# Rows spread over the partitions by a selector matmul and a VectorE copy instead of a DRAM round trip, in the mLSTM phase of a two-layer mixer

## The chip, the core and the metric

The program runs on one core of one Trainium2 chip. The metric is the device time of one execution, in microseconds. TensorE is the matmul engine (PE in the rows, its weight loads PEld), VectorE is DVE, ScalarE is ACT, GpSimd is POOL, and SyncE (SP) issues the DMAs.

## The reference, cut to what matters

The model has 512 tokens and 1024 channels. Its first mixer holds an mLSTM with 4 heads and a gated delta rule with 4 heads, both chunked; the input projections of both come from one normalised input. What the change touches are rows with one number for each head and token (4 x 512), which every partition needs:

```
b = jnp.cumsum(lf_, -1)                                     # mLSTM, log forget gates
log_d = where(causal, b[..., :, None] - b[..., None, :] + ig_[..., None, :], -inf)
m_t = jnp.maximum(jnp.max(log_d, -1), b + m[..., None])      # running maximum
d = jnp.exp(log_d - m_t[..., None])
...
G = jnp.cumsum(to_chunks(g, L), -1)                          # delta rule, log decays
decay = where(incl, exp(G[..., :, None] - G[..., None, :]), 0.0)
a_mat = where(strict, bc[..., :, None] * kk * decay, 0.0) + eye(L)   # bc = beta
```

The kernel computes with the token index on the free axis, so `d` and `decay` need a row of M (the running maximum), G and beta on all 128 partitions.

## The kernel before, in words

The program is a sequence of phases, each a block of five instruction streams that ends in a barrier: input loads and norm, `mlstm`, `delta`, the output projection, a feed-forward phase, a second mixer and its feed-forward phase, and a third layer. Nothing of a phase starts before every engine has left the one before. The order on each engine is the order in which the code is written; engines wait for each other by semaphores.

A projection of 128 output channels is 8 units of three matmuls each (`product`, L187 to L189: the fp32 weight and input are split into a high and a low part), 128x512 each. The split of the weight is a ScalarE copy (L151) and a subtraction on GpSimd or VectorE (L160); the 512 KB weight tile comes by SP's queue into a ring of four.

`mlstm` works head by head. In `body(h)` TensorE makes the attention scores of head h (`score`, L1619, banks b4 and b5), multiplies them with the values (`numerator`, L1626), turns tiles with 128x128 transposes (L204), and between these works through 24 units (16 from head 2 on) of the projections of later heads; `fill(n)` takes the next n units. VectorE takes the projections out of PSUM, weighs the scores (L1872), makes the arguments of the decays from the row M (`arguments`, L1864), and after a head takes its output (`out`, L1896). ScalarE exponentiates the arguments (L1719), GpSimd masks them (L1802).

The gate rows are made at the start of the phase as tiles of 4 partitions (`gate_rows`: M, G, beta). Head 0's row of M is spread to 128 partitions by TensorE: `spread_row` (L1604) multiplies a selector of ones with the four rows into a bank, and `take_m` (L1857) copies the bank to `m_M`. The rows of M for heads 1 to 3 and all rows of G and beta go through DRAM: SP's queue stores them to `row_scratch` (L1562, L1566, L1568) and loads them back with the partition axis broadcast (L1554), M into `m_M_next`, G and beta into `delta_bc`, which the `delta` phase reads. `turn_rows` (L1600) also turns G and beta into columns (`gate_cols`), from which L1926 to L1928 and L1931 make decay columns, with two ScalarE exponentials (L1765, L1766).

Of the kernel before, what the change touches and what calls it, by code (L numbers as in the profile page):

```python
# [86 lines left out]
class Core:  # L87
# [33 lines left out]
    def sem(self, name):  # L121
        self.sems.append(self.nc.alloc_semaphore(name))
        return self.sems[-1]
# [1371 lines left out]
def mlstm(k, weights, ahead):  # L1495
# [14 lines left out]
    acc, vraw, on, bcm = (sb(f"m_{s}", [P, T], F32) for s in "acc v_raw on M".split())  # L1510
    bcms = sb("m_M_next", [P, H - 1, T], F32)
    rows = nc.dram_tensor("row_scratch", (3 * HA, T), F32).ap()
    (rows_out, m_in, gb_in) = (sem("row_" + s) for s in ("out", "m_in", "gb_in"))
    q, kk = (sb(f"m_{s}", [DK, T], F32) for s in "q k".split())
# [10 lines left out]
    gb = lambda i: k.p("gbias", i)[0:HA]  # L1525
    (raw_taken, if_ready, tanh_done, f_soft, ab_taken, a_soft, b_ready, m_rows, g_rows, m_turned, m_cols, e_ready, g_turned,
     cols_ready, cols_exp, cols_done) = (sem("ab_" + s) for s in (
         "raw_taken if_ready tanh_done f_soft ab_taken a_soft b_ready m_rows g_rows m_turned m_cols e_ready g_turned "
         "cols_ready cols_exp cols_done").split())
    (qk_taken, og_taken, v_taken, v_turned, v_ready, v_ones, tapped, convolved, qk_ready, og_clamped, og_ready, m_spread, bcm_ready, arg_ready, d_ready,  # L1530
     d_masked, st_done, wt_ready, num_done, den_taken, squared, tot_ready, on_scaled, o_turned, y_ready, ch_act, ch_dve, ch_pool) = (sem("m_" + s) for s in (
         "qk_taken og_taken v_taken v_turned v_ready v_ones tapped convolved qk_ready og_clamped og_ready m_spread bcm_ready arg_ready d_ready "
         "d_masked st_done wt_ready num_done den_taken squared tot_ready on_scaled o_turned y_ready ch_act ch_dve ch_pool").split())

    def cs(c):
# [12 lines left out]
    with nc.Block() as block:  # L1548
        @block.sync
        def _(sp):  # L1550
            def spread_rows(out, kind, first, done):
                n = HA - first
                src = rows[kind * HA + first:(kind + 1) * HA, :].rearrange("(a h) t -> a h t", a=1).to_broadcast([P, n, T])
                sp.dma_start(out, src).then_inc(done, 16)  # L1554

            for h in range(2, H):
                for s in range(3):
                    k.wait_split(sp, 3 * h - 3 + s)
                    k.load(sp, s, weights[3 * h + s, :, :])
                if h == 2:  # L1560
                    sp.wait_ge(m_rows, 1)
                    sp.dma_start(rows[0:HA, :], r_M).then_inc(rows_out, 16)  # L1562
                    sp.wait_ge(rows_out, 16)
                    spread_rows(bcms[:, :, :], 0, 1, m_in)
                    sp.wait_ge(g_rows, 1)
                    sp.dma_start(rows[HA:2 * HA, :], r_G).then_inc(rows_out, 16)  # L1566
                    sp.wait_ge(b_ready, 1)
                    sp.dma_start(rows[2 * HA:3 * HA, :], r_b).then_inc(rows_out, 16)  # L1568
                    sp.wait_ge(rows_out, 48)
                    spread_rows(k.bcg[:, 0, :, :], 1, 0, gb_in)  # L1570
                    spread_rows(k.bcg[:, 1, :, :], 2, 0, gb_in)
            k.wait_split(sp, 3 * H - 1)
            k.load_ahead(sp, ahead, upto=3 * H)

        @block.tensor
        def _(pe):
# [52 lines left out]
            def body(h):  # L1629
                n, f = h + 1, h + 2  # L1630
                slots = {H: (0, 1), H + 1: (2, 3)}.get(f, (0, 1, 2))
                units = [(min(f, H), s, m) for s in slots for m in range(KD)]

                def fill(count):
                    for _ in range(min(count, len(units))):
                        g, s, m = units.pop(0)
                        project(g, s, m, m + 1)

                pe.wait_ge(qk_ready, h + 1)
                if h == 0:  # L1640
                    pe.wait_ge(bcm_ready, 1)
                if h == 1:
                    pe.wait_ge(cols_ready, 1)
                if h:
                    pe.wait_ge(y_ready, h - 1)
                score(h, 0)
                score(h, 1)
                fill(3)
                score(h, 2)
                score(h, 3)  # L1650
                fill(3)
                pe.wait_ge(v_ready, h + 1)
                if h:
                    pe.wait_ge(on_scaled, h)
                if h == 0:
                    pe.wait_ge(m_cols, 1)
                    pe.wait_ge(v_ones, 1)
                numerator(h, 0)
                numerator(h, 1)
                fill(2)  # L1660
                numerator(h, 2)
                numerator(h, 3).then_inc(num_done, 1)
                if n < H:
                    turn_v(n)
                if h:
                    turn_o(h - 1)
                fill(4)
                if h == 0:
                    pe.wait_ge(g_rows, 1)
                    pe.wait_ge(b_ready, 1)  # L1670
                    turn_rows(b4, (r_G, r_b)).then_inc(g_turned, 1)
                fill(len(units))

# [13 lines left out]
        def _(act):  # L1687
# [50 lines left out]
            def body(h):  # L1738
# [22 lines left out]
                if f < H:  # L1761
                    high(f + 1, 0)
                if h == 2:
                    act.wait_ge(cols_done, 1)
                    nc.scalar.activation(k.cols[:, 3, :, :], k.cols[:, 3, :, :], ACT.Exp)  # L1765
                    nc.scalar.activation(k.cols[:, 4:6, :, :], k.cols[:, 4:6, :, :], ACT.Exp, scale=-1.0).then_inc(cols_exp, 1)  # L1766
# [56 lines left out]
        def _(dve):  # L1823
# [30 lines left out]

            def take_m():
                dve.wait_ge(m_spread, 1)
                nc.vector.tensor_copy(bcm[:, :], b4[:, :]).then_inc(bcm_ready, 1)  # L1857

            def arguments(h):

                dve.wait_ge(*((m_in, 16) if h else (bcm_ready, 1)))
                m = bcms[:, h - 1, :] if h else bcm
                for j in range(NT):
                    ins = nc.vector.tensor_scalar(Ws[h % 2][:, off[j]:off[j + 1]], m[:, j * P:T], mcols[:, 0, h, j:j + 1], 0.0, ALU.subtract, ALU.max)  # L1864
                ins.then_inc(arg_ready, 1)
# [32 lines left out]
            def body(h):  # L1898
# [13 lines left out]
                take_den(h)  # L1912
                if n < H:
                    arguments(n)
                totals(h)
                if h:
                    out(h - 1)
                if h == 0:
                    dve.wait_ge(g_turned, 1)
                    t = b4[:, 0:2 * NT * HA].rearrange("p (k c h) -> p k h c", k=2, c=NT)  # L1920
                    nc.vector.tensor_copy(k.cols[:, 1:3, :, :], t).then_inc(cols_ready, 1)
                if h == 1:
                    dve.wait_ge(gb_in, 32)
                    dve.wait_ge(cols_ready, 1)
                    last = k.bcg[:, 0, :, :].rearrange("p h (c l) -> p h c l", l=P)[:, :, :, P - 1]
                    nc.vector.tensor_copy(k.cols[:, 5, :, :], last)  # L1926
                    ch.link(nc.vector.tensor_tensor(k.cols[:, 3, :, :], k.cols[:, 1, :, :], last, ALU.subtract))
                    nc.vector.tensor_copy(k.cols[:, 4, :, :], k.cols[:, 1, :, :]).then_inc(cols_done, 1)  # L1928
                if h == 3:
                    dve.wait_ge(cols_exp, 1)  # L1930
# [25 lines left out]
            dve.wait_ge(m_cols, 1)  # L1956
            take_m()
            arguments(0)
# [1324 lines left out]
```

## Time and profile before

| what | value |
|---|---|
| time, median of 3 runs | 1823.6 us (1821.07 to 1826.46) |
| time of the profiled execution | 1823.6 us |
| span of the profiled execution (first to last instruction) | 1821.8 us |
| TensorE busy | 1727.1 us, 95% |
| VectorE, ScalarE, GpSimd busy | 1080.8, 853.9, 428.9 us |
| TensorE clock granted, mean | 0.984 of full |
| the `mlstm` phase in the span | about 36 to 139 us |

A busy share is an average over all phases; what counts for the change is which engine sets the pace between 36 and 139 us. Matmuls are pipelined: their rows overlap, and the distance between two starts is what a matmul costs, not the duration in its row. A row's duration includes the time until the result has landed.

### The profile page before, as it was taken

The numbers are of one execution on the slowest core, as the hardware profiler recorded it, in microseconds if no ns is written. First come the engines' busy times: TensorE is split into PE (matmuls) and PEld (weight loads), VectorE is DVE, ScalarE is ACT, GpSimd is POOL, SyncE is SP. The second block draws the span as 40 slices with busy tenths as digits, with TensorE's granted clock in tenths as the row PEclk, the third lists the DMA queues.
The fourth block names the chain that finished last, engine by engine and source line by source line (L and its number), as shares of the span: only waits on it lengthen the run. The fifth ranks groups of instructions, "written<-read, shape, count | busy, mean of one in ns | idle before, by whom it ended". The sixth has DMA issues, their size and how long they took to land. (4 is left out here: it accounts for less than half of the span.)

```text
span 1821.8 us, 23819 instructions
## 1 busy us (share of the span) xinstructions
PE 1727.1 (95%) x8324; PEld 1394.1 (77%) x8324; DVE 1080.8 (59%) x1694; ACT 853.9 (47%) x1452; POOL 428.9 (24%) x332
## 2 busy tenths in 40 slices
PE   7998998989999999889999999999999989898997
PEld 5776887878888888768888877888888766666665
DVE  5536454377656633777887858566643475776243
ACT  5656445354333323565565645333332452445653
POOL 0434444101111100145555500111100111222222
PEclk9999999999999999999999999999999999999999
DMA  5311102223222222212212121323232320211111
GB/s 204 118 58 70 35 36 64 70 75 105 94 102 92 94 100 94 81 58 70 70 47 70 59 92 58 104 92 99 73 115 94 112 74 12 81 47 47 59 69 46
DMA packets 40360, 143.19 MB, mean 79 GB/s; under 512 B 4556, under 2 KB 4812, under 8 KB 39896
## 3 DMA queue, kind: packets, MB, share of 16 engines
q1 hardware_dynamic: 40280, 142.14, 23.0%
q8 instruction: 49, 0.80, 0.2%
q14 instruction: 31, 0.25, 0.0%
HBM read 140.00 MB, written 2.12 MB: 78 GB/s over the span
## 5 line engine op out<-in xcount | busy, mean ns | idle before, releaser
L187 PE MATMUL bank<-u_high,w_high 128*128 128x512 f32 x1580 | 650.6, 412 | 24.3 <-POOL w_low L160 10.0
L189 PE MATMUL bank<-u_high,w_low 128*128 128x512 f32 x1580 | 622.3, 394 | 0.0
L188 PE MATMUL bank<-u_low,w_high 128*128 128x512 f32 x1580 | 621.7, 393 | 0.0
L187 PEld LDWEIGHTS bank<-u_high,w_high 128*128 128x128 f32 x1580 | 300.6, 190 | 107.4 <-issue 31.7
L189 PEld LDWEIGHTS bank<-u_high,w_low 128*128 128x128 f32 x1580 | 299.7, 190 | 65.7
L151 ACT ACTIVATE w_high<-w_ring 128x1024 fp32r<-128x1024 f32 x233 | 244.0, 1052 | 221.4 <-PE bank L189 167.6
L188 PEld LDWEIGHTS bank<-u_low,w_high 128*128 128x128 f32 x1580 | 301.0, 191 | 58.4 <-issue 3.8
L160 DVE TENSOR_TENSOR w_low<-w_ring,w_high 128x1024 fp32r<-128x1024 f32 x176 | 220.9, 1258 | 178.3 <-ACT w_high L151 178.0
L160 POOL TENSOR_TENSOR w_low<-w_ring,w_high 128x1024 fp32r<-128x1024 f32 x57 | 135.7, 2391 | 532.7 <-ACT w_high L151 532.7
L881 ACT ACTIVATE conv_up<-bank,col_sb 128x512 f32<-128x512 f32 x88 | 68.6, 779 | 270.6 <-DVE bank L936 270.6
L996 POOL TENSOR_TENSOR hidden<-conv_up 128x512 f32 x44 | 58.2, 1323 | 494.0 <-DVE conv_up L947 373.8
L936 DVE TENSOR_TENSOR bank<-bank,root_in 128x512 f32<-128x512 f32 x88 | 61.4, 698 | 134.2 <-PE bank L189 133.5
L187 PE MATMUL bank<-src_high_down,w_high 128*128 128x512 f32 x352 | 137.5, 391 | 2.3 <-DVE src_low_down L479 2.3
L188 PE MATMUL bank<-src_low_down,w_high 128*128 128x512 f32 x352 | 137.2, 390 | 0.0
L189 PE MATMUL bank<-src_high_down,w_low 128*128 128x512 f32 x352 | 137.1, 390 | 0.0
L1319 POOL TENSOR_TENSOR c_X<-c_k,c_dif 128x256 f32<-128x256 f32 x56 | 60.0, 1071 | 150.9 <-ACT c_dif L1210 150.9
L187 PEld LDWEIGHTS bank<-src_high_down,w_high 128*128 128x128 f32 x352 | 66.1, 188 | 17.5 <-issue 2.2
L189 PEld LDWEIGHTS bank<-src_high_down,w_low 128*128 128x128 f32 x352 | 66.1, 188 | 13.7
L188 PEld LDWEIGHTS bank<-src_low_down,w_high 128*128 128x128 f32 x352 | 66.1, 188 | 13.5
L946 DVE SCALAR_TENSOR_TENSOR conv_up<-bank,col_sb,conv_up 128x511 f32<-128x511 f32 x88 | 65.9, 749 | 15.5 <-ACT conv_up L881 11.9
L947 DVE SCALAR_TENSOR_TENSOR conv_up<-bank,col_sb,conv_up 128x510 f32<-128x510 f32 x88 | 65.9, 749 | 10.1 <-DVE conv_up L946 0.3
L1354 DVE TENSOR_TENSOR c_dif<-c_G 128x512 f32<-128x512 f32 x56 | 54.5, 997 | 24.9 <-PE bank L1116 24.4
(414 smaller groups left out, 2294.8 us busy)
## 6 DMA issues: line engine op xcount, KB each, us to landing
w_ring<-ffn_up SPq DMA_DIRECT2D x88, 512.0 KB, 3.4
w_ring<-ffn_down SPq DMA_DIRECT2D x44, 512.0 KB, 3.4
w_ring<-c_in SPq DMA_DIRECT2D x32, 512.0 KB, 3.5
w_ring<-g_in SPq DMA_DIRECT2D x16, 512.0 KB, 3.6
w_ring<-m_in SPq DMA_DIRECT2D x12, 512.0 KB, 6.3
w_ring<-fox_in SPq DMA_DIRECT2D x12, 512.0 KB, 3.5
w_ring<-dsa_in SPq DMA_DIRECT2D x12, 512.0 KB, 3.4
w_ring<-ab_out SPq DMA_DIRECT2D x8, 512.0 KB, 4.1
```

The lines of the kernel that those rows point to most:

```text
L151: self.nc.scalar.activation(self.ws[s][0][:, :], self.w[:, s, :], ACT.Copy).then_inc(self.w_high, 1)
L160: eng.tensor_tensor(low[:, :], self.w[:, s, :], high[:, :].bitcast(F32), ALU.subtract).then_inc(self.w_split, 1)
L187: nc.tensor.matmul(out, a[0], b[0], start=start, stop=False)
L188: nc.tensor.matmul(out, a[0], b[1], start=False, stop=False)
L189: return nc.tensor.matmul(out, a[1], b[0], start=False, stop=stop)
L881: nc.scalar.activation(cg[:, s, :], bank(i, s)[:, :], ACT.Identity, bias=coef(4 * i + s, 3), scale=coef(4 * i + s, 2)).then_inc(tap_done, 1)
L936: nc.vector.tensor_tensor(bank(i, s)[:, :], bank(i, s)[:, :], k.rn[:, :], ALU.mult).then_inc(taken, 1)
L946: ch.link(nc.vector.scalar_tensor_tensor(cg[:, s, 1:T], bank(i, s)[:, 0:T - 1], coef(4 * i + s, 1), cg[:, s, 1:T], ALU.mult, ALU.add))
L947: nc.vector.scalar_tensor_tensor(cg[:, s, 2:T], bank(i, s)[:, 0:T - 2], coef(4 * i + s, 0), cg[:, s, 2:T], ALU.mult, ALU.add).then_inc(con ...
L996: nc.gpsimd.tensor_tensor(h[:, bass.ds(2 * i + s // 2, 1), :], cg[:, s - 1:s, :], cg[:, s:s + 1, :], ALU.mult).then_inc(mul_done, 1)
L1319: nc.gpsimd.tensor_tensor(x[:, :, 0, :], blocks(kk[:, :], b)[:, :, 0, :], d[:, :, 0, :], ALU.mult)
L1354: nc.vector.tensor_tensor(dif[:, l % R, :].rearrange("p (n b) -> p n b", b=2 * b), g, ref, ALU.subtract).then_inc(diff_ready, 1)
```

## The change

The DRAM scratch, SP's six DMAs on it with their three semaphores, and the tile `m_M_next` are gone. In their place:

- rows of M: after the last numerator of head h TensorE spreads the row of head h+1 into bank b5, and VectorE copies it to `m_M` before it makes the arguments;
- rows of G and beta: each of the 8 is spread into b4 or b5 by TensorE near the end of a body, behind two units of `fill`, and copied to `delta_bc` by VectorE: four rows in head 0 (all of G), two in head 1 and two in head 2;
- the next head's first scores wait until the last copy has left the bank (`spread_used`);
- the decay columns are made one head earlier on VectorE and ScalarE.

The core of the diff. In order: SP, the lists, TensorE in `body(h)` (ahead of the scores, behind the last numerator, ahead of the last fill), ScalarE's exponentials of the columns, VectorE:

```diff
-                if h == 2:
-                    sp.wait_ge(m_rows, 1)
-                    sp.dma_start(rows[0:HA, :], r_M).then_inc(rows_out, 16)
-                    sp.wait_ge(rows_out, 16)
-                    spread_rows(bcms[:, :, :], 0, 1, m_in)
...
-                    spread_rows(k.bcg[:, 0, :, :], 1, 0, gb_in)
-                    spread_rows(k.bcg[:, 1, :, :], 2, 0, gb_in)
...
+    spreads = {0: [(0, h) for h in range(H)], 1: [(1, 0), (1, 1)], 2: [(1, 2), (1, 3)], 3: []}
+    used = {h: sum(len(spreads[g]) for g in range(h)) for h in range(H + 1)}
...
-                if h == 0:
-                    pe.wait_ge(bcm_ready, 1)
-                if h == 1:
-                    pe.wait_ge(cols_ready, 1)
+                pe.wait_ge(bcm_ready, h + 1)
+                pe.wait_ge(spread_used, used[h])
...
                 if n < H:
+                    pe.wait_ge(wt_ready, NT * h + NT)
+                    spread_row(b5, r_M, n).then_inc(m_spread, 1)
...
+                for i, (kind, g) in enumerate(spreads[h]):
+                    fill(2)
+                    if i == 0:
+                        pe.wait_ge(*((y_ready, h) if h else (cols_ready, 1)))
+                    elif i == 1:
+                        pe.wait_ge(bcm_ready, n + 1)
+                    else:
+                        pe.wait_ge(spread_used, used[h] + i - 1)
+                    spread_row(b_s[i % 2], (r_G, r_b)[kind], g).then_inc(spread, 1)
                 fill(len(units))
...
-                if h == 2:
+                if h == 1:
...
-            def take_m():
-                dve.wait_ge(m_spread, 1)
-                nc.vector.tensor_copy(bcm[:, :], b4[:, :]).then_inc(bcm_ready, 1)
+            def take_m(h):
+                dve.wait_ge(m_spread, h + 1)
+                nc.vector.tensor_copy(bcm[:, :], (b5 if h else b4)[:, :]).then_inc(bcm_ready, 1)
...
                 if n < H:
+                    take_m(n)
                     arguments(n)
...
-                if h == 1:
-                    dve.wait_ge(gb_in, 32)
-                    dve.wait_ge(cols_ready, 1)
+                for i, (kind, g) in enumerate(spreads[h]):
+                    dve.wait_ge(spread, used[h] + i + 1)
+                    nc.vector.tensor_copy(k.bcg[:, kind, g, :], b_s[i % 2][:, :]).then_inc(spread_used, 1)
+                if h == 0:
+                    dve.wait_ge(spread_used, H)
```

TensorE, the last part of body(2) in the kernel before, from the last numerator of head 2 to the first scores of head 3 (L1626 numerator, L204 transposes, L187 a unit's first matmul, L1619 scores):

```order
L1626 MATMUL bank7<-m_v0,x_res 128x129 x3
L204 MATMUL bank2<-cst_sb,m_v_raw 128x128 [waits m_v_taken]
...
L204 MATMUL bank4<-cst_sb,m_on 128x128 [waits m_y_ready,m_on_scaled]
...
L187 MATMUL bank1<-u_high,w1_high 128x512 [waits m_og_taken,w_split]
...
L1619 MATMUL bank4<-m_q,m_k 128x512 [waits m_y_ready,m_qk_ready]
L1619 MATMUL bank5<-m_q,m_k 128x384
```

The same place in the changed kernel, whose line numbers are others (L1608 numerator, L1586 `spread_row`, L1601 scores):

```order
L1608 MATMUL bank7<-m_v0,x_res 128x129 x3
L1586 MATMUL bank5<-gate_rows,cst_sb 128x512 [waits m_wt_ready]
L204 MATMUL bank2<-cst_sb,m_v_raw 128x128 [waits m_v_taken]
...
L204 MATMUL bank4<-cst_sb,m_on 128x128 [waits m_y_ready,m_on_scaled]
...
L187 MATMUL bank1<-u_high,w1_high 128x512 [waits m_og_taken,w_split]
...
L1586 MATMUL bank4<-gate_rows,cst_sb 128x512 [waits m_y_ready]
...
L1586 MATMUL bank5<-gate_rows,cst_sb 128x512 [waits m_bcm_ready]
L1601 MATMUL bank4<-m_q,m_k 128x512 [waits ab_spread_used,m_y_ready,m_bcm_ready,m_qk_ready]
L1601 MATMUL bank5<-m_q,m_k 128x384
```

Eight units (24 matmuls) stood between the transposes and the scores; now six stand before the first of the two spreads, two between them, and none behind the second, so that the scores' wait for `spread_used` follows it directly. In heads 0 and 1 four and eight units stand behind the last spread.

VectorE behind head 0 in the kernel before (L1877 takes the denominators, L1864 makes the arguments of head 1):

```order
L1877 COPY m_den<-bank7 128x2
L1864 TENSOR_SCALAR x_res<-m_M_next,m_cols 128x512 [waits row_m_in]
L1864 TENSOR_SCALAR x_res<-m_M_next,m_cols 128x384
L1864 TENSOR_SCALAR x_res<-m_M_next,m_cols 128x256
L1864 TENSOR_SCALAR x_res<-m_M_next,m_cols 128x128
```

And in the changed kernel (L1868, L1849 `take_m`, L1855 the arguments, L1916 the copies to `delta_bc`):

```order
L1868 COPY m_den<-bank7 128x2
L1849 COPY m_M<-bank5 128x512 [waits m_m_spread]
L1855 TENSOR_SCALAR x_res<-m_M,m_cols 128x512 [waits m_bcm_ready]
...
L1913 COPY gate_cols<-bank4 128x32 [waits ab_g_turned]
L1916 COPY delta_bc<-bank4 128x512 [waits ab_spread]
L1916 COPY delta_bc<-bank5 128x512 [waits ab_spread]
L1916 COPY delta_bc<-bank4 128x512 [waits ab_spread]
L1916 COPY delta_bc<-bank5 128x512 [waits ab_spread]
L1920 COPY gate_cols<-delta_bc 128x16 [waits ab_spread_used]
```

A copy that waits for the spread now stands ahead of the arguments, and four copies ahead of the column work.

## Rows read from the trace of the kernel before

**Rows 1.** The page: busy time, share, instructions of each engine.
```profile
PE 1727.1 (95%) x8324; PEld 1394.1 (77%) x8324; DVE 1080.8 (59%) x1694; ACT 853.9 (47%) x1452; POOL 428.9 (24%) x332
```
**Rows 2.** Busy time by stretch: us, engines' busy (instructions), TensorE clock, DMA share.
```profile
core 0: us, PE busy (x) PEld busy (x) DVE busy (x) ACT busy (x) POOL busy (x), PEclk, DMA share, GB/s
57.50:81.30 23.80, 22.94 (x113) 17.87 (x112) 9.49 (x22) 14.87 (x29) 13.71 (x9) 1.00 0.41 155
81.30:103.80 22.50, 22.50 (x109) 17.81 (x108) 9.19 (x25) 13.60 (x27) 8.86 (x7) 1.00 0.34 117
103.80:120.80 17.00, 17.00 (x85) 13.31 (x84) 8.82 (x22) 13.28 (x29) 6.47 (x6) 1.00 0.10 32
139.00:300.00 161.00, 146.39 (x907) 125.42 (x908) 82.89 (x140) 87.28 (x197) 75.09 (x69) 0.99 0.13 47
```
**Rows 3.** Timeline of TensorE, end of `mlstm`: start us, us, instruction, idle before.
```profile
137.47 0.60 PE L204 MATMUL bank<-cst_sb,m_on 128*128 128x128 f32 x4
139.25 0.47 PE L187 MATMUL bank<-u_high,w_high 128*128 128x512 f32 x1 [1.18 <-PEq L1548]
```
**Rows 4.** Timeline of SP's queue and of VectorE, the DRAM way and its readers.
```profile
57.01 0.82 SPq L1554 DMA_DIRECT2D delta_bc<-row_scratch  x2
60.17 5.23 SPq L127 DMA_DIRECT2D w_ring<-m_in  x3
...
69.32 0.23 DVE L1877 COPY m_den<-bank 128x2 f32<-128x2 f32 x2 [2.68 <-PE bank L1626]
69.47 1.26 DVE L1864 TENSOR_SCALAR x_res<-m_M_next,m_cols 128x512 f32<-128x512 f32 x4
```
**Rows 5.** Timeline of TensorE, the spread of head 0's row.
```profile
47.68 1.12 PE L1604 MATMUL bank<-gate_rows,cst_sb 4*128 4x512 f32 x2 [0.22 <-DVE gate_rows L1947]
48.64 0.60 PE L1600 MATMUL bank<-cst_sb,gate_rows 4*128 4x4 f32 x8
```
**Rows 6.** Timeline of TensorE, scores of head 1 between two units.
```profile
80.84 0.39 PE L188 MATMUL bank<-u_low,w_high 128*128 128x512 f32 x1
81.07 0.39 PE L189 MATMUL bank<-u_high,w_low 128*128 128x512 f32 x1
81.39 1.77 PE L1619 MATMUL bank<-m_q,m_k 64*128 64x512 f32 x4
83.09 0.50 PE L187 MATMUL bank<-u_high,w_high 128*128 128x512 f32 x1
83.42 0.40 PE L188 MATMUL bank<-u_low,w_high 128*128 128x512 f32 x1
```
**Rows 7.** Timelines of TensorE and VectorE: a result, its reader, a copy from PSUM.
```profile
72.42 0.65 PE L1600 MATMUL bank<-cst_sb,gate_rows 4*128 4x4 f32 x8
...
73.11 0.19 DVE L1921 COPY gate_cols<-bank 128x32 f32<-128x32 f32 x1 [1.72 <-PE bank L1600]
...
46.95 0.68 DVE L1947 TENSOR_TENSOR gate_rows<-gate_rows 4x512 f32<-4x512 f32 x1
...
50.31 0.69 DVE L1857 COPY m_M<-bank 128x512 f32<-128x512 f32 x1
```
**Rows 8.** Timelines of GpSimd and VectorE: slack behind heads 0 and 2.
```profile
72.57 1.70 POOL L1802 TENSOR_TENSOR x_res<-x_res,cst_sb 128x128 f32<-128x128 f32 x4 [7.53 <-ACT x_res L1719]
...
82.62 0.69 DVE L1872 SCALAR_TENSOR_TENSOR x_res<-bank,x_res 128x512 f32<-128x512 f32 x1 [9.31 <-PE bank L1619]
...
122.16 1.16 DVE L1872 SCALAR_TENSOR_TENSOR x_res<-bank,x_res 128x512 f32<-128x512 f32 x2 [4.29 <-PE bank L1619]
```
**Rows 9.** Timelines of TensorE and GpSimd: the one stall inside the heads.
```profile
60.20 0.50 PE L187 MATMUL bank<-u_high,w_high 128*128 128x512 f32 x1 [0.86 <-POOL w_low L160]
...
53.70 2.63 POOL L1802 TENSOR_TENSOR x_res<-x_res,cst_sb 128x128 f32<-128x128 f32 x4 [10.12 <-ACT x_res L1719]
```
**Rows 10.** Timeline of TensorE at the start of `mlstm`: matmuls at the lower clock.
```profile
37.14 0.77 PE L187 MATMUL bank<-u_high,w_high 128*128 128x512 f32 x1 [3.25 <-DVE m_on L1934]
...
40.22 0.40 PE L188 MATMUL bank<-u_low,w_high 128*128 128x512 f32 x1
```

More of the change, by code:

```diff
@@ L1510, in mlstm @@
     acc, vraw, on, bcm = (sb(f"m_{s}", [P, T], F32) for s in "acc v_raw on M".split())
-    bcms = sb("m_M_next", [P, H - 1, T], F32)
-    rows = nc.dram_tensor("row_scratch", (3 * HA, T), F32).ap()
-    (rows_out, m_in, gb_in) = (sem("row_" + s) for s in ("out", "m_in", "gb_in"))
     q, kk = (sb(f"m_{s}", [DK, T], F32) for s in "q k".split())
@@ L1525, in mlstm @@
     gb = lambda i: k.p("gbias", i)[0:HA]
-    (raw_taken, if_ready, tanh_done, f_soft, ab_taken, a_soft, b_ready, m_rows, g_rows, m_turned, m_cols, e_ready, g_turned,
+    (raw_taken, if_ready, tanh_done, f_soft, ab_taken, a_soft, b_ready, m_rows, g_rows, m_turned, m_cols, e_ready, g_turned, spread, spread_used,
      cols_ready, cols_exp, cols_done) = (sem("ab_" + s) for s in (
-         "raw_taken if_ready tanh_done f_soft ab_taken a_soft b_ready m_rows g_rows m_turned m_cols e_ready g_turned "
+         "raw_taken if_ready tanh_done f_soft ab_taken a_soft b_ready m_rows g_rows m_turned m_cols e_ready g_turned spread spread_used "
          "cols_ready cols_exp cols_done").split())
@@ L1550, in _ @@
         def _(sp):
[L1551 to L1554, printed above, removed]
             for h in range(2, H):
@@ L1559, in _ @@
                     k.load(sp, s, weights[3 * h + s, :, :])
-                if h == 2:
-                    sp.wait_ge(m_rows, 1)
-                    sp.dma_start(rows[0:HA, :], r_M).then_inc(rows_out, 16)
-                    sp.wait_ge(rows_out, 16)
-                    spread_rows(bcms[:, :, :], 0, 1, m_in)
[L1565 to L1569, printed above, removed]
-                    spread_rows(k.bcg[:, 0, :, :], 1, 0, gb_in)
-                    spread_rows(k.bcg[:, 1, :, :], 2, 0, gb_in)
             k.wait_split(sp, 3 * H - 1)
@@ L1663, in body @@
                 if n < H:
+                    pe.wait_ge(wt_ready, NT * h + NT)
+                    spread_row(b5, r_M, n).then_inc(m_spread, 1)
+                if n < H:
                     turn_v(n)
@@ L1853, in convolve @@
                 ins.then_inc(convolved, 1)
-            def take_m():
-                dve.wait_ge(m_spread, 1)
-                nc.vector.tensor_copy(bcm[:, :], b4[:, :]).then_inc(bcm_ready, 1)
+            def take_m(h):
+                dve.wait_ge(m_spread, h + 1)
+                nc.vector.tensor_copy(bcm[:, :], (b5 if h else b4)[:, :]).then_inc(bcm_ready, 1)
             def arguments(h):
-                dve.wait_ge(*((m_in, 16) if h else (bcm_ready, 1)))
-                m = bcms[:, h - 1, :] if h else bcm
+                dve.wait_ge(bcm_ready, h + 1)
                 for j in range(NT):
-                    ins = nc.vector.tensor_scalar(Ws[h % 2][:, off[j]:off[j + 1]], m[:, j * P:T], mcols[:, 0, h, j:j + 1], 0.0, ALU.subtract, ALU.max)
+                    ins = nc.vector.tensor_scalar(Ws[h % 2][:, off[j]:off[j + 1]], bcm[:, j * P:T], mcols[:, 0, h, j:j + 1], 0.0, ALU.subtract, ALU.max)
                 ins.then_inc(arg_ready, 1)
@@ L1928, in body @@
                     nc.vector.tensor_copy(k.cols[:, 4, :, :], k.cols[:, 1, :, :]).then_inc(cols_done, 1)
-                if h == 3:
+                if h == 2:
                     dve.wait_ge(cols_exp, 1)
@@ L1956, in _ @@
             dve.wait_ge(m_cols, 1)
-            take_m()
+            take_m(0)
             arguments(0)
```

## The prediction

> **What bounds the kernel now.** I read the page first: TensorE is busy 1727.1 of 1821.8 us, 95%, and no other engine passes 59% [rows 1]. That is an average over eleven phases, so the busy time by stretch comes next, cut at the first scores of each head. In the stretches of heads 0 to 2 TensorE is busy 22.94 of 23.80, 22.50 of 22.50 and 17.00 of 17.00 us, at full clock; VectorE is busy for less than half of the first two and 8.82 of 17.00 in the third [rows 2]. The reader is to see that in the place of the change TensorE has no hole to put work in: two stretches of the three have none, the first has one stall of 0.86 us, ahead of all added work but not made by it [rows 9].
>
> The timeline then says who wants what the DRAM way delivers. The broadcast of G and beta is issued at 57.01 and the M rows are there when VectorE turns to them: it makes the arguments at 69.47, right behind the denominators, with no wait for a DMA [rows 4]. The SP queue, free of these DMAs at 57.83, next issues a weight load at 60.17, and that one waits for a split. It follows GpSimd's low part, not the row DMAs. So what is removed is hidden entirely, and what is added lies mainly on the engine that sets the pace.
>
> **What is removed.** Six DMAs on SP's queue, worth nothing: nobody is seen waiting for them, and SP is held by the weight splits anyway [rows 4]. One possible gain is left: their traffic may slow other engines. GpSimd's first mask took 2.63 us against 1.70 us in the next head [rows 8, 9], and the stall of 0.86 us waits for GpSimd's work behind it. VectorE was busy with the gate rows at that moment too, so I take 0 and keep -0.86 us as the end of the range.
>
> **One spread on TensorE.** Two matmuls of 512 columns, 4 partitions deep. Head 0's spread stands in the trace: it starts at 47.68 and the next instruction at 48.64, so it costs 0.96 us inside a run of plain fp32 matmuls [rows 5]. Between units of projections the change of kind costs too. The scores of head 1 start 0.32 us after the unit matmul before them, where units follow each other at 0.23 us: 0.09 us. The second matmul behind the scores comes at 0.33 us: 0.10 us [rows 6]. An isolated spread is 0.96 + 0.19 = 1.15 us. Below, it can't be less than the 0.96 us of the row, as long as it runs; above, I use its 1.12 us from start to the landed result, if nothing of it overlapped, plus 0.19, so 1.31 us.
>
> - The three M spreads (heads 1 to 3) stand between the numerator and the transposes, fp32 on both sides: 3 x 0.96 = 2.88 us.
> - Of the eight spreads of G and beta, seven stand alone between units (four in head 0, two in head 1, the first in head 2): 7 x 1.15 = 8.05 us.
> - The eighth stands directly ahead of the scores of head 3 and shares their entry: 0.96 us.
>
> **The waits added.** Behind the eighth spread no unit is left. The scores wait for `spread_used`, so: the result lands 1.12 us after the spread's start, VectorE sees it 0.04 us later (73.07 to 73.11), the copy takes 0.69 us, and TensorE starts 0.05 us after VectorE ends (47.63 to 47.68) [rows 5, 7]. That makes 1.90 us after the spread's start, where the scores could have started at 0.96: a new stall of 0.94 us. Below it is 0; above 1.90 us. Queued behind this wait are the scores of head 3 and all units after them, so nothing covers it.
>
> The other waits I cost at nothing. Two units, six matmuls at 0.23 us, are 1.4 us between spreads, more than the 0.94 us that the copy lags, and a bank is used again only at the second next spread. Behind the last spread of heads 0 and 1 stand four and eight units. The wait for `y_ready` has six units ahead of it. If one of these covers were gone, it would cost up to 0.94 us each.
>
> **VectorE, ScalarE, GpSimd.** VectorE gets 11 copies of 0.69 us, 7.6 us in all, into stretches where it waits 9.31 us ahead of the first weighing of head 1 and 4.29 us ahead of that of head 3 [rows 7, 8]. The M copy stands ahead of the arguments: at latest it ends at 69.32 + 1.12 + 0.04 + 0.69 = 71.17, so the arguments come 1.7 us later, and the exponentials and the mask with them. The mask of head 1 ended at 74.27 and is wanted at 82.62, which itself moves out by more than 5 us [rows 4, 8]. Nothing is late there: 0.
>
> **The sum.** 2.88 + 8.05 + 0.96 + 0.94 = 12.8 us, against the profiled execution's own 1823.6 us (span 1821.8 and 1.8 around it), which is also the median of the three runs. `mlstm` ends with TensorE's last transposes at 137.47, VectorE's output behind them, and a barrier; TensorE starts again at 139.25 [rows 3]. All phases behind it move out by the same amount: 1836.4 us.
>
> **The rivals.**
>
> *The clock falls.* Eleven more changes of kind, one new stall, and spreads that use four partitions of 128. For it: before `mlstm` TensorE stood still for 3.25 us, and its next eight starts, 37.14 to 40.22, took 3.08 us for seven distances that are 1.6 us at 0.23: the lower level, 1.2 GHz, for 1.5 us of loss [rows 10]. Against it: after the idle stretches of 0.86 and 1.18 us the next unit matmuls come at full clock, and heads 0 to 2 show 1.00 throughout, with four or more such groups in each [rows 2, 3, 9]. One spell in each of three heads: 12.8 + 4.5 = 17.3, 1840.9 us. The Trainium skill (TensorE: Matmul & The Clock Gate, "A second HAM failure mode: psum-queue depth-cycling") warns that short idle moments between groups of matmuls that cycle through PSUM banks can make the clock swing between its levels; that speaks against this change, and the granted clock of 1.00 in heads that already cycle through eight banks does not bear it out.
>
> *The copies are always late.* If VectorE reaches each spread late, or a wait costs TensorE its run-ahead, each of the seven other spreads exposes 0.94 us: 12.8 + 6.6 = 19.4, 1843.0 us. For it: VectorE runs in order and the copies stand behind totals and output. Against it: the 9.31 us of slack, and 1.4 us between two spreads.
>
> *Not slower: the end of `mlstm` isn't TensorE's.* If another engine comes last to the barrier by 12.8 us or more, the added work vanishes under it, and the stall of 0.86 us may go with the DMAs: 1823.6 - 0.9 = 1822.7 us. It decides at the barrier, at the point where that engine's lateness equals the sum. For it: 14.6 us of the 161 us behind are idle on TensorE, so something else is waited for in `delta` [rows 2]. Against it: the only work between 137.47 and 139.25 hangs on TensorE's own transposes, and units of the next projection follow at once [rows 3]. Idle time behind a barrier covers nothing ahead of it.
>
> **How the numbers follow.** The forecast has 80%, the clock 8%, the late copies 6%, the covered end 6%. For the range: the low end has eleven spreads at 0.96, no new stall and the old one gone, 10.56 - 0.86 = 9.7 us; the high end eleven at 1.31 and 1.90 of stall, 16.3 us. With the 2.9 us by which runs of the kernel before lie around their median, that is 1830.4 to 1842.8; I take 1831 to 1842, which holds the clock's case and leaves out the other two. About 0.3%, or 5.5 us, is what can be told from no change. The forecast is 0.7%, and its low bound of 9.7 us still counts as slower; the covered end counts as the same. So slower 0.92, same 0.06, faster 0.02, the last for what no case here names.
>
> **What would show it.** In the changed kernel: 22 matmuls of 4x512 on the line of `spread_row` beyond the first two, 0.96 us to the next start beside fp32 work and 1.15 us beside units; TensorE idle for about 0.9 us ahead of the scores of head 3 and for nothing ahead of those of heads 1 and 2; the last transposes of `mlstm` at 150.3 instead of 137.5, and the distance from there to the end unchanged; the granted clock 1.00 in all three heads. By heads, TensorE's first scores would lie later by 0.96 + 4 x 1.15 = 5.6 us (head 1), 8.8 us (head 2) and 12.8 us (head 3). The stall of 0.86 us at 60 should stay. I'd be wrong if the first scores of head 1 came less than 5 us later, which would mean a spread is cheaper than its row; if the phases behind `mlstm` gave time back; or if the clock column fell below 1.00.

## The result, and the profile after

| | kernel before | changed kernel |
|---|---|---|
| median (5 runs each) | 1823.6 us (1818.06 to 1826.46) | 1840.08 us (1835.05 to 1844.43) |
| ratio | | 1.0092, 95% interval 1.0074 to 1.0111 |
| profiled execution, span | 1821.8 us | 1837.0 us |

The change costs 0.9%. The time lies inside the forecast range of 1831 to 1842, at 16.5 us of excess where 12.8 were forecast. The page of the changed kernel has 22 more matmuls and 11 more VectorE instructions than [rows 1]:

```profile
PE 1741.9 (95%) x8346; PEld 1395.7 (76%) x8346; DVE 1090.7 (59%) x1705; ACT 854.3 (47%) x1452; POOL 428.8 (23%) x332
```

The busy time by stretch of the changed kernel, cut at the first scores of heads 1, 2 and 3 and at the start of `delta` (columns as in [rows 2]):

```profile
57.50:87.70 30.20, 29.34 (x123) 19.04 (x122) 13.49 (x30) 15.06 (x29) 13.71 (x9) 1.00 0.16 53
87.70:114.00 26.30, 26.30 (x116) 18.56 (x115) 10.96 (x25) 13.82 (x29) 8.87 (x7) 1.00 0.33 120
114.00:135.60 21.60, 20.63 (x91) 14.14 (x91) 11.21 (x26) 14.54 (x28) 9.69 (x8) 1.00 0.00 1
135.60:157.00 21.40, 20.27 (x85) 14.89 (x85) 5.71 (x13) 2.70 (x14) 1.49 (x1) 0.84 0.00 0
```

Against 23.80, 22.50 and 17.00 us of the kernel before, the first three stretches are 6.4, 3.8 and 4.6 us longer, at full clock. The fourth took 18.32 us before (120.93 to 139.25) and takes 21.36 now, with a granted clock of 0.84. Nothing was added there. TensorE's timeline in that place of the changed kernel says what happened:

```profile
133.19 0.39 PE L189 MATMUL bank<-u_high,w_low 128*128 128x512 f32 x1
133.51 1.12 PE L1586 MATMUL bank<-gate_rows,cst_sb 4*128 4x512 f32 x2
135.62 3.07 PE L1601 MATMUL bank<-m_q,m_k 64*128 64x512 f32 x4 [0.99 <-DVE delta_bc L1916]
138.62 0.80 PE L187 MATMUL bank<-u_high,w_high 128*128 128x512 f32 x1
139.21 0.63 PE L188 MATMUL bank<-u_low,w_high 128*128 128x512 f32 x1
139.63 0.63 PE L189 MATMUL bank<-u_high,w_low 128*128 128x512 f32 x1
...
142.75 0.92 PE L1601 MATMUL bank<-m_q,m_k 64*128 64x256 f32 x4
```

The reader is to see three things: the eighth spread at 133.51; the stall of 0.99 us behind it, which ends with VectorE's copy; and then scores that take 3.00 us to the next start instead of the 1.70 of [rows 6], and units 0.43 us apart instead of 0.23. That is the lower clock, 1.2 GHz, as in [rows 10]. It lasts until about 142.7 us and costs 21.36 - 18.32 = 3.04 us.

The spreads themselves, in head 0 of the changed kernel:

```profile
69.17 1.12 PE L1586 MATMUL bank<-gate_rows,cst_sb 4*128 4x512 f32 x2
70.22 0.66 PE L204 MATMUL bank<-cst_sb,m_v_raw 128*128 128x128 f32 x4
...
78.41 1.12 PE L1586 MATMUL bank<-gate_rows,cst_sb 4*128 4x512 f32 x2
79.46 0.50 PE L187 MATMUL bank<-u_high,w_high 128*128 128x512 f32 x1
80.28 0.40 PE L187 MATMUL bank<-u_high,w_high 128*128 128x512 f32 x1
81.06 1.12 PE L1586 MATMUL bank<-gate_rows,cst_sb 4*128 4x512 f32 x2
```

The next start comes 1.05 us after the spread's, where [rows 5] have 0.96. From spread to spread it is 81.06 - 78.41 = 2.65 us, of which two units (each three matmuls, one start every 0.23 us) take 1.38: an isolated spread costs 1.27 us, not 1.15. `delta` starts at 156.98 instead of 139.25, 17.7 us later [rows 3]; at the end of the span the difference is 15.2 (1837.0 against 1821.8), because two later phases, whose code is the same, took less time at a higher granted clock in this execution (238.2 us at 0.98 against 239.0 at 0.97, and 115.4 at 0.99 against 117.5 at 0.96). Such differences occur between executions of one kernel too (1682.8 and 1679.1 us behind the phase in the two profiles of the kernel with units behind the last spread), so from here on I compare the `mlstm` phase in the traces and use whole times only as a bound.

### The profile page after: what moved, and what is told of

Same layout as the page of the kernel before. It is cut to its first block and busy times, and to the rows that moved or that the text cites. A ratio compares the mean times of both kernels' runs of the same rounds, so it can differ in the third digit from the quotient of the medians.

```text
span 1837.0 us, 23870 instructions
## 1 busy us (share of the span) xinstructions
PE 1741.9 (95%) x8346; PEld 1395.7 (76%) x8346; DVE 1090.7 (59%) x1705; ACT 854.3 (47%) x1452; POOL 428.8 (23%) x332
## 5 line engine op out<-in xcount | busy, mean ns | idle before, releaser
L187 PE MATMUL bank<-u_high,w_high 128*128 128x512 f32 x1580 | 650.4, 412 | 24.2 <-POOL w_low L160 9.9
L187 PEld LDWEIGHTS bank<-u_high,w_high 128*128 128x128 f32 x1580 | 300.5, 190 | 113.8 <-issue 37.5
L187 PE MATMUL bank<-src_high_down,w_high 128*128 128x512 f32 x352 | 137.3, 390 | 2.3 <-DVE src_low_down L479 2.3
L187 PEld LDWEIGHTS bank<-src_high_down,w_high 128*128 128x128 f32 x352 | 66.1, 188 | 17.5 <-issue 2.2
L189 PEld LDWEIGHTS bank<-src_high_down,w_low 128*128 128x128 f32 x352 | 66.1, 188 | 13.7
L947 DVE SCALAR_TENSOR_TENSOR conv_up<-bank,col_sb,conv_up 128x510 f32<-128x510 f32 x88 | 65.9, 748 | 10.1 <-DVE conv_up L946 0.3
```

Of the source, the lines that this page charges most:

```text
L187: nc.tensor.matmul(out, a[0], b[0], start=start, stop=False)
L189: return nc.tensor.matmul(out, a[1], b[0], start=False, stop=stop)
L947: nc.vector.scalar_tensor_tensor(cg[:, s, 2:T], bank(i, s)[:, 0:T - 2], coef(4 * i + s, 0), cg[:, s, 2:T], ALU.mult, ALU.add).then_inc(con ...
```

## The experiments

Because the `mlstm` phase starts a little earlier or later in each execution, the table counts from head 0's first scores to the start of `delta`, and from head 3's first scores to there. "At 1.2 GHz" is the excess of the second column over 18.3.

| kernel | head 0 to `delta` | head 3 to `delta` | at 1.2 GHz | ratio to before, interval |
|---|---|---|---|---|
| before | 81.7 | 18.32 | - | 1 |
| changed | 99.5 | 21.36 | 3.0 | 1.0092 (1.0074 to 1.0111) |
| changed again | 99.4 | 21.34 | 3.0 | 1.0079 (1.0048 to 1.0110) |
| units behind the last spread | 95.3 | 18.26 | none | 1.0094 (1.0078 to 1.0111) |
| the same again | 95.5 | 18.26 | none | one run |
| M only | 85.3 | 18.32 | none | 1.0030 (1.0016 to 1.0044) |
| G and beta only | 94.1 | 19.74 | 1.4 | 1.0081 (1.0061 to 1.0100) |
| DRAM way beside it | 99.5 | 21.37 | 3.0 | 1.0081 (1.0050 to 1.0112) |
| stall alone, 0.79 us | 82.5 | 18.32 | none | 1.0014 (1.0002 to 1.0026) |
| the same again | 81.7 | 18.32 | none | one run |
| stall alone, 2.43 us | 87.3 | 21.43 | 3.1 | one run |
| spreads doubled | 117.5 | 19.75 | 1.4, and more in heads 0 and 1 | 1.0192 (1.0159 to 1.0225) |
| extra matmul, 128 rows | 104.6 | 19.75 | 1.4 | one run |
| split rows | 93.0 | 18.25 | none there, one spell in head 0 | 1.0063 (1.0044 to 1.0083) |

My theory after the first comparison: the spreads cost 1.2 to 1.3 us each on TensorE, the stall 1.0, and the stall brought the lower clock. The rival: the clock fell by chance or for the spreads' sake.

**Units behind the last spread.**

```diff
-                    fill(2)
+                    fill(1 if h == 2 else 2)
```

> Same work as the changed kernel, but in head 2 one unit stands ahead of each of the two spreads instead of two, so that two units (1.4 us) stand behind the last. My theory: the 0.99 us stall ahead of head 3's scores goes, and with it the stretch at the lower clock that came right behind it (about 3.1 us); the kernel is about 4 us faster than the changed one and 13.6 us slower than the one before, 3 x 1.19 + 8 x 1.26. Rival: the lower clock has nothing to do with the stall and comes anyway (or came by chance): then only 1.0 us goes, and the clock column below 1.00 shows somewhere between the scores of head 2 and the end of the phase.

The stall and the lower clock are both gone, and the phase is 4.1 us shorter (95.3 against 99.5); the second profile below says the same. So the stall was the trigger or part of it. In whole time the 4 us can't be seen: the ratio of 1.0094 is no better than the changed kernel's, and its interval, 14.2 to 20.2 us over the kernel before, lies above the 13.7 us expected. The expectation missed for the median and held for the phase.

**M only.** From the kernel before: M's store and broadcast out, `spread_row` and `take_m(h)` in, G and beta left to SP.

```diff
-                    spread_rows(bcms[:, :, :], 0, 1, m_in)
...
+                    spread_row(b5, r_M, n).then_inc(m_spread, 1)
...
+                    take_m(n)
```

> Only the three rows of M go by TensorE and VectorE; G and beta keep the DRAM way. My theory: three spreads inside fp32 runs at 1.19 us each, as the changed kernel's trace has them, 3.6 us over the kernel before (about 1827.2), no stall and no lower clock. Rival: what costs is the chain M copy, arguments, exponentials, mask coming 1.5 us later, which would show as TensorE waits ahead of scores or numerators, and more than 5 us.

81.7 became 85.3: 3.7 us for three spreads, 1.22 each, no stall. The chain of M copy, arguments and mask, 1.7 us later, makes nobody wait. The rival falls.

**G and beta only.** From the changed kernel: M back to the DRAM way.

```diff
-                    spread_row(b5, r_M, n).then_inc(m_spread, 1)
...
+                    sp.dma_start(rows[0:HA, :], r_M).then_inc(rows_out, 16)
+                    sp.wait_ge(rows_out, 16)
+                    sp.dma_start(bcms[:, :, :], src).then_inc(m_in, 16)
```

> Only the eight rows of G and beta go by TensorE and VectorE; M keeps the DRAM way. My theory: 7 x 1.26 + 1.05 + 0.99 of stall + 3.1 at the lower clock = 14.0 us over the kernel before, and this and the M-only kernel's excess add up to the changed kernel's in the phase (17.8 us). Rival: the lower clock needs both parts; then 10.9 us and a clock of 1.00 behind the stall.

94.12 - 81.67 = 12.45 us, of which 1.4 at the lower clock instead of 3.1, so 11.0 without it, against 10.9 expected. The parts add up: 3.7 + 11.0 + 3.0 = 17.7. The lower clock needs no M spreads, and the length of its spell varies.

**The stall alone.** In the kernel before, with the DRAM way, TensorE waits ahead of head 3's scores for a copy that VectorE makes of the last unit's bank. The edit also moves the last unit out of the loop of `fill`, in the same place and order.

```diff
+                    pe.wait_ge(pause_done, 1)
...
+                    nc.vector.tensor_copy(spare[:, :], k.ps[1][:, :]).then_inc(pause_done, 1)
```

> The kernel before, DRAM way and all, with one thing added: ahead of head 3's scores TensorE waits for a 128x512 VectorE copy of the last unit's result (about 0.95 us of stall), which nobody reads. My theory: the stall itself brings the lower clock, so this costs 0.95 + about 3 us = 4 us, and scores at twice their duration follow it. Rival: the clock fell because the 4-partition spreads had kept the array nearly unused; then the stall costs 0.95 us alone and the clock stays 1.00.

A miss: the phase grew by 0.9 us and the clock stayed.

```profile
120.73 0.39 PE L189 MATMUL bank<-u_high,w_low 128*128 128x512 f32 x1
121.91 1.77 PE L1621 MATMUL bank<-m_q,m_k 64*128 64x512 f32 x4 [0.79 <-DVE spare L1938]
123.60 0.50 PE L187 MATMUL bank<-u_high,w_high 128*128 128x512 f32 x1
```

The scores take their usual 1.69 us. So a stall of this length was not enough here; in the changed kernel it is 0.2 us longer and a spread stands ahead of it. That leaves two questions: is it the time without a 128-row matmul (there 133.6 to 135.6, here 121.1 to 121.9), or chance?

**The changed kernel again**, unedited.

> The changed kernel once more, unedited, for a second profile. The stretch at the lower clock behind the stall was seen in the changed kernel (3.0 us) and in the G-and-beta-only kernel (1.4 us), and not behind a stall of 0.8 us alone. Theory A: the spread of 4 partitions and the stall together bring it, so it comes again here, with a length that varies (1 to 3.5 us). Theory B: it is chance: then it is gone and the next phase starts 14.7 us later than in the kernel before instead of 17.7.

It came again, 3.0 us of loss. With the G-and-beta, DRAM-beside and 128-row kernels, all five profiled executions that have the eighth spread ahead of this stall show it, 1.4 or 3.0 us of loss, and so does the doubled kernel's (1.4). None of the seven executions without that pair and without the longer stall below (the kernel before, M only, split rows, and two each with units behind and with the short stall) shows it in this place. Chance alone is a poor account of that, so theory B falls; but the length varies among equal stalls.

**A longer stall alone.** Three dependent copies in place of the one, and a short one of 4 columns that gives the signal.

```diff
-                    nc.vector.tensor_copy(spare[:, :], k.ps[1][:, :]).then_inc(pause_done, 1)
+                    for _ in range(3):
+                        ins = nc.vector.tensor_copy(spare[:, :], k.ps[1][:, :])
+                        ch.link(ins)
+                    ins = nc.vector.tensor_copy(spare[:, 0:4], k.ps[1][:, 0:4]).then_inc(pause_done, 1)
```

> The kernel before with a longer stall ahead of head 3's scores: TensorE waits for three dependent VectorE copies, about 2.4 us instead of 0.8, as long as TensorE in the changed kernel goes without a full matmul (from 133.6 to 135.6). Theory A1: what counts is how long the array is without full-height work; the lower clock comes here too, and the next phase starts 2.4 us + 1 to 3.5 us later than in the kernel before. Theory A2: it needs the spreads themselves; then the start moves by 2.4 us alone and the clock stays 1.00.

```profile
124.69 3.35 PE L1621 MATMUL bank<-m_q,m_k 64*128 64x512 f32 x4 [2.43 <-DVE spare L1941]
127.98 0.79 PE L187 MATMUL bank<-u_high,w_high 128*128 128x512 f32 x1
128.57 0.63 PE L188 MATMUL bank<-u_low,w_high 128*128 128x512 f32 x1
129.00 0.63 PE L189 MATMUL bank<-u_high,w_low 128*128 128x512 f32 x1
```

The lower clock comes without any spread, for 3.1 us of loss, so A2 falls: spreads are not needed. It is one profile, and it does not show that the length of an idle stretch decides. About 15 us into `delta` TensorE has an idle stretch of 2.2 us in every kernel here, and the two profiles of the short stall, one and the same kernel, differ behind it. The first two lines are of the first profile, the last two of the second (columns as in the timelines and in [rows 2]):

```profile
155.35 1.16 PE L2095 MATMUL bank<-g_k 128*128 128x128 f32 x8 [2.22 <-DVE g_q L2533]
155.35:159.20 3.85, 3.85 (x27) 3.59 (x28) 1.84 (x3) 1.33 (x6) 3.30 (x4) 1.00 0.08 31
155.49 1.86 PE L2095 MATMUL bank<-g_k 128*128 128x128 f32 x8 [2.21 <-DVE g_q L2533]
155.49:159.20 3.71, 3.71 (x18) 3.71 (x19) 0.66 (x2) 0.00 (x0) 2.30 (x2) 0.54 0.10 41
```

After 2.22 us the clock stays at 1.00, after 2.21 us it falls (0.54). In the kernel before, idle stretches of 2.19 us (ahead of 154.37) and of 3.64 us (ahead of 1458.41) both end at full clock. So an idle stretch makes a fall possible, and what decides whether it comes stays open.

**The DRAM way beside the new one**, into a tile nobody reads.

```diff
+                    sp.dma_start(rows[0:HA, :], r_M).then_inc(rows_out, 16)
...
+                    spread_rows(0, 1, 3)
...
+                    spread_rows(1, 0, 3)
+                    sp.wait_ge(m_in, 32)
+                    spread_rows(2, 0, 3)
```

> The changed kernel, and beside it the DRAM way again, into a tile that nobody reads (three stores and three broadcasts, 2.25 MB instead of 2.75 MB, each broadcast waiting for the one before). My theory: the DRAM way was hidden, so nothing changes in the phase: the first scores at 57.5 and 87.7, the stall of 0.86 us before 60.2 still there. Rival: its traffic had slowed GpSimd or the weight loads, and removing it gave something back that the added work hid; then the phase here is 0.5 us or more longer than the changed kernel's up to head 3's scores.

99.5 us again, and the stall of 0.86 us is still there. What the change removed was worth nothing in this phase, to 0.1 us.

**The spreads doubled.**

```diff
+                    spread_row(b_s[i % 2], (r_G, r_b)[kind], g)
                     spread_row(b_s[i % 2], (r_G, r_b)[kind], g).then_inc(spread, 1)
```

> The changed kernel with each of the eight G and beta spreads issued twice into the same bank. My theory: TensorE's own time sets the price, so each second one costs 0.96 us (two plain fp32 matmuls inside a run): 7.7 us more up to head 3's scores (143.3 instead of 135.6), and nothing else moves. Rival: part of the 1.26 us is the wait or the change of kind that another matmul can lie under; then under 6 us.

A miss on the other side, and the most telling run: 1858.0 us, 18 us over the changed kernel. Head 0 alone took 44.7 us instead of 30.2, where four more spreads should take 3.8.

```profile
76.14 1.98 PE L1586 MATMUL bank<-gate_rows,cst_sb 4*128 4x512 f32 x4
78.05 0.50 PE L187 MATMUL bank<-u_high,w_high 128*128 128x512 f32 x1
78.39 0.43 PE L188 MATMUL bank<-u_low,w_high 128*128 128x512 f32 x1
78.62 0.63 PE L189 MATMUL bank<-u_high,w_low 128*128 128x512 f32 x1
79.04 0.63 PE L187 MATMUL bank<-u_high,w_high 128*128 128x512 f32 x1
...
80.45 3.78 PE L1586 MATMUL bank<-gate_rows,cst_sb 4*128 4x512 f32 x4
```

Its busy time from 76 to 102.6 us, in the columns of [rows 2]:

```profile
76.00:102.60 26.60, 26.60 (x47) 13.06 (x46) 3.21 (x7) 1.52 (x2) 4.69 (x2) 0.55 0.00 0
```

TensorE is busy for 26.60 of 26.60 us, and its granted clock is 0.55. It fell while the engine never stood still: the start at 78.62 comes 0.23 us behind the one before it, as at full clock, and the next one 0.42 us later. So the fall comes 0.6 us behind 1.9 us of matmuls on 4 partitions. Head 1 has a second spell (granted clock 0.94 over its 29.7 us).

The rows also give the bare price of the two matmuls. Four of them take 78.05 - 76.14 = 1.91 us to the next start, two take 1.05 (above), so a spread behind another costs 0.86 us.

**A full-height extra.** As the doubled kernel, but the extra matmul reads 128 partitions.

```diff
+                    nc.tensor.matmul(b_s[i % 2][:, :], k.c("ones"), k.rn[:, :], start=True, stop=True)
                     spread_row(b_s[i % 2], (r_G, r_b)[kind], g).then_inc(spread, 1)
```

> The changed kernel with one extra plain fp32 matmul of 128 partitions x 512 columns ahead of each of the eight G and beta spreads, into the same bank, overwritten by the spread. It takes TensorE as long as the second spread of the doubled kernel did (0.96 us), but with all 128 rows of the array in use. Theory H (the height counts): TensorE's time grows by 8 x 0.96 = 7.7 us and the clock stays 1.00 in heads 0 and 1; the first scores of head 1 stand 30.2 + 3.8 = 34.0 us after those of head 0 instead of 44.7 in the doubled kernel. Theory F (plain fp32 groups of that length bring the lower clock, whatever their height): about 44 us again.

Head 0 took 33.5 us (34.0 expected by H, 44 by F), and the clock stayed at 1.00 in heads 0 to 2, with about the same time on TensorE in the same places. Its timeline and its busy time:

```profile
76.89 0.39 PE L189 MATMUL bank<-u_high,w_low 128*128 128x512 f32 x1
77.12 1.02 PE L1663 MATMUL bank<-root_in,cst_sb 128*128 128x512 f32 x2
78.07 1.12 PE L1586 MATMUL bank<-gate_rows,cst_sb 4*128 4x512 f32 x2
79.12 0.50 PE L187 MATMUL bank<-u_high,w_high 128*128 128x512 f32 x1
79.45 0.39 PE L188 MATMUL bank<-u_low,w_high 128*128 128x512 f32 x1
```

```profile
75.00:92.50 17.50, 17.50 (x61) 9.61 (x60) 3.40 (x8) 3.52 (x9) 6.45 (x6) 1.00 0.00 0
```

The extra also multiplies other numbers, `ones` with `root_in`, where a selector is nearly all zeros. That the height and not the values kept the clock up is the likelier reading; no run separates the two, and each of the two kernels has one profile.

The run also shows where the entry cost comes from. The plain fp32 matmul with 128 rows starts 0.23 us after a projection's matmul, with no gap. To the spread behind it are 0.95 us, the bare 0.86 and a step of 0.09. The spread takes 1.05 us to the next start, and the second start behind it comes at 0.33. The 0.1 us steps belong to the change from 128 rows to few and back, not to the change of type. There are four of them around an isolated spread, one at each of the two starts behind a change: 0.86 + 4 x 0.10 = 1.26 us.

**Split rows.** Spreads as two one-pass matmuls on high and low parts.

```diff
+                nc.tensor.matmul(bank[:, :], s, Rh[:, kind, :], start=True, stop=False)
+                return nc.tensor.matmul(bank[:, :], s, Rl[:, kind, :], start=False, stop=True)
...
+            for i, r in enumerate((r_M, r_G, r_b)):
+                ins = nc.vector.tensor_tensor(Rl[:, i, :], r, Rh[:, i, :].bitcast(F32), ALU.subtract)
```

> The kernel with two units behind the last spread, and the spreads made cheaper: rows and selector stand as high and low parts in the matmuls' one-pass type, as the projections do, so a spread is two matmuls of 512 columns at 0.23 us and not two at 0.48. VectorE makes the parts of M, G and beta once, GpSimd the selector's. Theory: 0.46 us each with no change of kind, 11 x 0.46 = 5.1 us in place of 13.7; the next phase starts 5 us after that of the kernel before, and the kernel is some 8.5 us faster than the one with fp32 spreads, still slower than the kernel before. Rival: so few rows of the array in use bring the lower clock also here, and more than 3 us of the gain goes.

Half a hit. Heads 1 and 2 take 25.0 and 19.6 us, 2.55 more than before for three spreads each: 0.85 us a spread, down from 1.26, not 0.46. The steps of 0.1 us at a change of height remain:

```profile
78.05 0.39 PE L189 MATMUL bank<-u_high,w_low 128*128 128x512 f32 x1
78.37 0.49 PE L1674 MATMUL bank<-rows_high,sel_high 4*128 4x512 f32 x1
78.70 0.39 PE L1675 MATMUL bank<-rows_low,sel_high 4*128 4x512 f32 x1
79.03 0.50 PE L187 MATMUL bank<-u_high,w_high 128*128 128x512 f32 x1
79.36 0.39 PE L188 MATMUL bank<-u_low,w_high 128*128 128x512 f32 x1
```

Four distances of 0.32 to 0.33 where units have 0.23. Head 0 has a second loss: VectorE's splitting of the rows took 5.8 us of its time around the first scores, the stall behind the scores grew from 0.86 to 1.25 us (that the one caused the other is not shown), and the clock fell there too (0.94 over head 0). The phase is 93.0, 11.3 over the kernel before where 5.1 were expected.

**Two second profiles**, of the kernel with units behind the last spread and of the short stall alone.

> The kernel with two units behind the last spread once more, for a second profile. Theory (the lower clock needs about 2 us without full-height matmuls): between the first scores of head 0 and the start of the next phase it takes 95.3 us again, 13.7 more than the kernel before, with a clock of 1.00. If the lower clock shows here, it isn't the stall that brings it.

95.5 us, full clock in the phase: it holds.

> The kernel before with the short stall (0.79 us) once more. Theory: 1.1 us without a full-height matmul doesn't bring the lower clock: 82.5 us from head 0's first scores to the next phase again, 0.9 more than before. If it takes 84 or more, a short stall does bring it at times, and the length of 2 us is no condition.

No lower clock behind this stall again: 18.32 us from head 3's scores. The 81.7 us from head 0's are 0.8 less than expected because in this execution head 0's first scores came later (58.64, not 57.70) and the stall of 0.86 us behind them is gone.

No variant that spreads rows by TensorE is as fast as the kernel before; in the phase the closest is M only, 3.7 us over it.

## Why the prediction was right, and where it was not

- **The bound.** Right: TensorE has no hole in heads 0 to 2 but the stall of 0.86 us, and what was put on it came out at the end. The starts of head 1, 2 and 3 moved by 6.35, 10.1 and 14.7 us; 5.6, 8.8 and 12.8 were forecast.
- **The removed DMAs, cost 0.** Shown by the kernel with the DRAM way beside: the same 99.5 us, and the 0.86 us stall is in both. The -0.86 us in the low end of the range has no support.
- **The M spreads, 3 x 0.96 = 2.88.** Mis-sized: 1.19 each in the trace (from the start of head 0's last row of numerators to the first unit, 3.11 us against 1.92), 1.22 in the M-only kernel, 3.6 in all. I read the 0.96 of [rows 5] as the price of the two matmuls. It is their 0.86 and one step of 0.10, because transposes of 4 rows, the same height, follow that spread; here 128-row matmuls stand on both sides. I put the extra down to a change of kind, and between fp32 neighbours took none. It is a change of height, as the full-height run shows.
- **The lone spreads, 7 x 1.15 = 8.05.** Mis-sized for the same reason: 1.27 each, 8.9 in all. The 0.19 us of entry and exit came from the scores [rows 6] and is right. It holds two of the four steps and the 0.96 holds a third; the fourth, at the start right behind the spread (1.05 for 0.96), is what the sum lacked.
- **The eighth, 0.96, and the stall, 0.94.** 2.11 us from its start to the scores, 1.90 forecast: landing 1.12 and copy 0.69 as in the rows, the stall 0.99 as the trace puts it. The scores start 0.26 us after the copy's end (135.36), where I took 0.05 from [rows 5]. Right within 0.2 us, and the unit reordering shows that it goes with two units behind it.
- **The other waits, VectorE, ScalarE, GpSimd, cost 0.** Right: no other wait of TensorE in heads 0 to 2 was added. The late copies' rival is not seen.
- **The clock, cost 0.** The step that failed. I wrote that after idle stretches of 0.86 and 1.18 us units come at full clock, and took that for the stall's evidence too. But ahead of this stall stands a spread on 4 partitions, and together it is 2.0 us. One spell with 3.0 us of loss came in both profiles of the changed kernel; the rival had one of 1.5 us in each of three heads, so it named the direction and not the place. By my own sign, a clock column below 1.00, the account was wrong, though heads 0 to 2 kept 1.00. The rival's rule in the Trainium skill (TensorE: Matmul & The Clock Gate, "A second HAM failure mode: psum-queue depth-cycling") blames short idle moments between groups that cycle through banks. The clock did swing, but cycling through banks did not do it, as heads 0 to 2 at 1.00 show, nor did one short idle moment of 0.8 us.
- **The covered end.** Not seen: the last transposes stand at 155.27 and `delta` follows 1.7 us behind, as before.

The trace's sum is 3.6 + 8.9 + 2.1 + 3.0 = 17.6 us, of 17.7 measured at the start of `delta`. The forecast missed 1.6 us of spreads, 0.2 of stall and 3.0 of clock. That the range held is in part luck. Its high end, 16.3 us, has a dear spread and a long stall but no clock; the 17.6 us of the trace lie beyond it, and it took the 2.9 us allowed for scatter, and a median of 16.5, to come out inside. What stays open is when a spell comes and how long it lasts: 1.4 us of loss in three executions, 3.0 in three, with the same spread and stall.

## What to carry to other kernels

A transfer that lands before its reader turns to it cost nothing here, for all its detour (99.5 us with and without it). Before such a transfer is replaced by instructions on another engine, look whether that engine has a hole at that place, and count each instruction by the distance between starts, with neighbours of the same height as it will have. Where a wait for another engine's copy must stand in a TensorE stream, leave full-height work behind the producer to cover it: in this phase that was worth 4 us for the exchange of two units, though the medians of the whole time do not show the gain.

## What the runs showed of the hardware

- TensorE can be busy without a gap and lose its clock: with 26.60 of 26.60 us busy the granted clock was 0.55 where doubled matmuls on 4 partitions stood between units, and 1.00 where the added matmuls used 128 partitions (one profile each; the added matmuls' values differ too).
- Ahead of the falls stood 1.9 us of 4-partition matmuls, 2.0 us of such a spread and idle time, or 2.2 or 2.4 us of idle time alone. Idle times of 0.8 us (two profiles of the short stall) and 1.2 us (start of `delta`) brought none. Length does not decide: 2.2 us brought a fall in one profile of the short-stall kernel and none in the other, and 3.64 us brought none in the kernel before. Scores on 64 partitions followed by the 0.86 us stall, 2.6 us in all, brought none either [rows 9]; with 1.25 us of stall behind them, in the split-rows kernel, the clock fell.
- A matmul of 512 columns in plain fp32, two instructions on the trace, takes 0.86 us of TensorE at full clock among neighbours of its own height. A change between 128 partitions and 4 adds about 0.10 us to each of the next two starts, so 0.4 us around an isolated spread, in the one-pass type (0.85 us for two matmuls of 0.23) as in plain fp32 (1.26). Going between these two types at 128 partitions costs nothing (0.23 us to the next start).
- A lower-clock spell nearly doubled units, from 0.23 to 0.43 us, and the scores, from 1.70 to 3.00, and cost 1.4 or 3.0 us.
